# Block inverse of the delta rule: the plain inverse as DVE's 32x32 block transpose of the transposed one

## The reference, cut to what matters

```python
a_strict = jnp.where(strict, jnp.einsum("bhncd,bhnmd->bhncm", kb, k) * decay, 0.0)
lower = jnp.eye(c, dtype=f32) + a_strict
rhs = jnp.concatenate([vb, kb * jnp.exp(g)[..., None]], axis=-1)
sol = lax.linalg.triangular_solve(lower, rhs, left_side=True, lower=True, unit_diagonal=True)
```

## Time and profile before

| | |
|---|---|
| profiled execution | 1562.33 us, span 1560.4 us |
| median of three runs | 1563.34 us |
| TensorE busy | 1401.4 us (90%) |
| DVE busy | 588.0 us (38%) |
| ScalarE busy | 301.3 us (19%) |
| GpSimd busy | 361.2 us (23%) |
| mean HBM traffic | 293 GB/s |
| mean granted TensorE clock | 0.955 of full |

### The profile page before, as it was taken

One profiled execution on the slowest core, in us unless ns is written; L12 is line 12 of the kernel. 1 busy time (PEld: TensorE's weight loads), 2 busy tenths in 40 slices (PEclk: granted clock), 3 DMA queues, 4 the chain that ended last, 5 costly groups with the idle time before them and its releaser, 6 DMA issues.

```text
span 1560.4 us, 33996 instructions
## 1 busy us (share of the span) xinstructions
PE 1401.4 (90%) x13302; PEld 661.4 (42%) x13303; DVE 588.0 (38%) x1331; ACT 301.3 (19%) x563; POOL 361.2 (23%) x421
## 2 busy tenths in 40 slices
PE   6998898979938999999999999989899988889982
PEld 3445555555413444444344443434333343334441
DVE  2688877753253222223222232222222223222231
ACT  3113232031211111112112121121111211111122
POOL 5001000010012123333223232222232223222332
PEclk9999999978958999999999999999999999999996
DMA  9212000040168799999999999999999999999995
GB/s 307 70 55 78 3 28 1 1 164 1 49 238 290 285 370 372 392 410 408 403 396 405 407 405 405 395 405 408 410 401 398 410 408 405 401 408 404 409 385 145
DMA packets 110262, 457.76 MB, mean 293 GB/s; under 512 B 15140, under 2 KB 36132, under 8 KB 77430
## 3 DMA queue, kind: packets, MB, share of 16 engines
q1 hardware_dynamic: 86566, 427.88, 68.6%
q0 software_dynamic: 20592, 27.68, 7.5%
q10 hardware_dynamic: 3072, 1.76, 0.4%
HBM read 439.05 MB, written 18.22 MB: 293 GB/s over the span
## 4 chain that ended last, share of the span: by engine, by line
PE 67%; DMA 12%; DVE 10%; SPq 6%; issue 2%; ACT 2%; POOL 0%; ACTq 0%; DVEq 0%; POOLq 0%
PE bank L1840 29%; PE bank L1882 15%; DMA ring<-in_w_gate_up_dram 11%; PE bank L1528 5%; PE bank L1702 4%; PE bank L1908 3%; SPq L369 3%; SPq L374 3%; PE bank L1812 2%; DVE dslots L973 2%; PE bank L1593 1%; DVE qkbuf L997 1%; PE bank L1523 1%; PE bank L1801 1%; PE bank L1601 1%
## 5 line engine op out<-in xcount | busy, mean ns | idle before, releaser
L1840 PE MATMUL bank<-ring,wq 128*32 128x512 f32 x5184 | 588.2, 607 | 38.3 <-DMA ring<-in_w_gate_up_dram 35.8
L1840 PEld LDWEIGHTS bank<-ring,wq 128*32 128x32 f32 x5184 | 163.7, 112 | 412.6 <-issue 411.8
L1882 PE MATMUL bank<-dslots,intra 128*32 128x256 f32 x5056 | 301.6, 381 | 4.4 <-issue 1.9
L1882 PEld LDWEIGHTS bank<-dslots,intra 128*32 128x32 f32 x5056 | 169.1, 110 | 117.3 <-issue 30.2
L856 ACT ACTIVATE wq<-bank 128x512 f32<-128x512 f32 x128 | 66.1, 602 | 626.5 <-PE bank L1840 626.5
L540 POOL DMA_INDIRECT acc_rows<-rows,idx_out x83 | 153.8, 1854 | 45.8 <-POOL idx_out L530 25.6
L1411 DVE TENSOR_TENSOR intra<-bank,small 128x256 f32<-128x256 f32 x128 | 45.3, 416 | 291.8 <-PE bank L1908 259.7
L1528 PE MATMUL bank<-hbuf,ring 128*128 128x512 f32 x320 | 147.2, 600 | 0.0
L1336 DVE TENSOR_TENSOR small<-consts,bank 128x4 f32<-128x4 f32 x34 | 5.4, 159 | 327.0 <-PE bank L1801 327.0
L530 POOL COPY idx_in<-idx 128x4 int32 (+1 forms) x34 | 6.3, 186 | 448.8 <-PE bank L1812 386.1
L535 POOL DMA_INDIRECT wq<-xn_rows,idx_in x88 | 88.1, 1001 | 45.4 <-POOL idx_in L530 27.5
(11 more groups left out here) (279 smaller groups left out, 1105.7 us busy)
## 6 DMA issues: line engine op xcount, KB each, us to landing
ring<-in_w_gate_up_dram SPq DMA_DIRECT2D x256, 1024.0 KB
dslots<-in_w_down_dram SPq DMA_DIRECT2D x124, 1024.0 KB
ring<-in_w_in_dram SPq DMA_DIRECT2D x12, 1024.0 KB
ring<-in_w_out_dram SPq DMA_DIRECT2D x4, 1024.0 KB
ring<-in_w_down_dram SPq DMA_DIRECT2D x4, 1024.0 KB
rows<-in_x_dram SPq DMA_DIRECT2D x4, 512.0 KB, 7.5
hbuf<-in_x_dram SPq DMA_DIRECT2D x4, 512.0 KB, 4.9
xn_rows<-convbuf POOLq DMA_DIRECT2D x4, 512.0 KB, 4.4
```

The source lines that it names most:

```text
L1840: ins = M(bank[g][GROUP * j:GROUP * (j + 1), :], xT[:, g, c % 2, (c // 2) * GROUP:(c // 2 + 1) * GROUP], w[:, :, j * QD:(j + 1) * QD], sta ...
L1882: ins = M(b[GROUP * j:GROUP * (j + 1), col:col + QD], actT[:, g, c % 2, (c // 2) * GROUP:(c // 2 + 1) * GROUP], w[:, cc, j * QD:(j + 1) * QD],
```

## The change

After the change one of the two forms of the inverse is always the DVE block transpose of the other: one instruction over the 128x512 buffer, which transposes each 32x32 block where it stands. XT at the start is the transpose of X (so step 4, TensorE's transpose of Am and the two DVE instructions at L1031 and L1033 are gone); at levels 2 to 16 X is the transpose of the new XT (so the product at L1599 and the subtraction at L1044 are gone). The wait of TensorE for X moves from the Am' XT product to the update product. Without step 4, the SiLU job of a head's first slot stands behind step 3 in DVE's queue instead of before it.

```diff
--- before.py
+++ after.py
@@ -309,6 +309,7 @@
             LAST_TILE[u] = max(LAST_TILE.get(u, 0), i)
         LAST_TILE[NU - 2] = LAST_TILE[NU - 1] = NT - 1
         GDN_STEPS = 16
+        XX_STEPS = 2 * len(LEVELS) - 1
         PER_SLOT = [5, 5, 6]
 
         def gdn_of(s):
@@ -1025,15 +1026,7 @@
                                        in1=sq[b], op0=ALU.mult, op1=ALU.mult).then_inc(norm_ready, 1)
 
             def level(h, s):
-                if s == 1:
-
-                    dve.wait_ge(p_done, 6 * h + 1)
-                    own.mark(V.tensor_tensor(Pm, view(bank[5], 0, T, P), bcm(lmask[1]), ALU.mult))
-                    own.settle()
-                    V.scalar_tensor_tensor(out=XT, in0=Pm, scalar=-1.0, in1=bcm(ident), op0=ALU.mult,
-                                           op1=ALU.add).then_inc(xx_ready, 1)
-                    return
-                dve.wait_ge(p_done, 6 * h + LEVELS.index(s) + 1)
+                dve.wait_ge(p_done, 5 * h + LEVELS.index(s))
                 V.tensor_tensor(Pm, view(bank[5], 0, T, P), bcm(lmask[s]), ALU.mult).then_inc(p_ready, 1)
 
             def level_x(h, s):
@@ -1041,7 +1034,9 @@
                 dve.wait_ge(xx_done, 5 * h + k)
                 V.tensor_tensor(XT, XT, view(bank[7], 0, T, P), ALU.subtract).then_inc(xx_ready, 1)
                 if s < LEVELS[-1]:
-                    V.tensor_tensor(X, X, view(bank[6], 0, T, P), ALU.subtract).then_inc(xx_ready, 1)
+
+                    dve.wait_ge(xx_ready, XX_STEPS * h + 2 * k + 1)
+                    V.transpose(X[:, :, :], XT[:, :, :]).then_inc(xx_ready, 1)
 
             def gdn(h, k):
                 if k == 0:
@@ -1085,6 +1080,8 @@
                     own.settle()
                     V.scalar_tensor_tensor(out=X, in0=X, scalar=-1.0, in1=bcm(ident), op0=ALU.mult,
                                            op1=ALU.add).then_inc(xx_ready, 1)
+                    dve.wait_ge(xx_ready, XX_STEPS * h + 1)
+                    V.transpose(XT[:, :, :], X[:, :, :]).then_inc(xx_ready, 1)
                 if k == 3:
                     dve.wait_ge(kv_turned, h + 1)
                     bct = lambda v: v[:, :, h:h + 1].to_broadcast([P, T, P])
@@ -1093,8 +1090,6 @@
                     own.mark(V.tensor_tensor(uval[:, h, :, :], view(bank[4], 0, T, P), bct(betah), ALU.mult))
                     own.settle()
                     dve.sem_inc(kv_ready, 1)
-                if k == 4:
-                    level(h, 1)
                 if 5 <= k < 15:
                     s = LEVELS[1 + (k - 5) // 2]
                     if k % 2 == 1:
@@ -1117,7 +1112,7 @@
                 if s >= 2:
                     if 0 in steps:
 
-                        steps = [0, 1, 2, 4, 3]
+                        steps = [0, 1, 2, 3]
                         jobs = [jobs[0], lambda: None, lambda: None, jobs[2], lambda: norm(s - 2), tap(1)]
                     elif steps:
                         jobs[1] = tap(1)
@@ -1550,7 +1545,7 @@
                     pe.wait_ge(bias_ready, 1)
                 if k == 0:
                     if h >= 1:
-                        pe.wait_ge(xx_ready, 11 * h)
+                        pe.wait_ge(xx_ready, XX_STEPS * h)
                     for t in range(T):
                         ins = M(bank[7][:, t * P:(t + 1) * P], gg[:, t, h:h + 1].to_broadcast([P, P]), triu,
                                 start=True, stop=True)
@@ -1576,33 +1571,26 @@
                     for t in range(T):
                         ins = TR(bank[4][:, t * P:(t + 1) * P], vT[:, t * P:(t + 1) * P], ident)
                     ins.then_inc(kv_turned, 1)
-                if k == 4:
+                if k == 5:
                     pe.wait_ge(a_ready, h + 1)
-                    for t in range(T):
-                        ins = TR(bank[5][:, t * P:(t + 1) * P], Am[:, t, :], ident)
-                    ins.then_inc(p_done, 1)
-                if k == 5:
                     pe.wait_ge(in_ready, h + 1)
                     pe.wait_ge(egb_ready, h + 1)
                 if 5 <= k < 15:
                     lv = 1 + (k - 5) // 2
-                    s = LEVELS[lv]
                     if k % 2 == 1:
-                        pe.wait_ge(xx_ready, 11 * h + 2 * lv)
+                        pe.wait_ge(xx_ready, XX_STEPS * h + (2 if lv == 1 else 2 * lv - 1))
                         for t in range(T):
                             ins = M(bank[5][:, t * P:(t + 1) * P], Am[:, t, :], XT[:, t, :], start=True, stop=True)
                         ins.then_inc(p_done, 1)
                     else:
+                        pe.wait_ge(xx_ready, XX_STEPS * h + 2 * lv)
                         pe.wait_ge(p_ready, 5 * h + lv)
-                        if s < LEVELS[-1]:
-                            for t in range(T):
-                                M(bank[6][:, t * P:(t + 1) * P], Pm[:, t, :], X[:, t, :], start=True, stop=True)
                         for t in range(T):
                             ins = M(bank[7][:, t * P:(t + 1) * P], X[:, t, :], Pm[:, t, :], start=True,
                                     stop=True)
                         ins.then_inc(xx_done, 1)
                 if k == 15:
-                    pe.wait_ge(xx_ready, 11 * h + 11)
+                    pe.wait_ge(xx_ready, XX_STEPS * h + XX_STEPS)
                     pe.wait_ge(kv_ready, h + 1)
                     pe.wait_ge(rs_ready, min(2 * (h + 1) + 2, 2 * H))
                     for t in range(T):
```

## The result

The changed kernel took 1545.98 us (median of four runs, 1543.04 to 1547.54) against 1563.62 for the kernel before beside it: ratio 0.9891, interval 0.9879 to 0.9904. The forecast was 1546.5; its distance of 0.5 us is smaller than the spread of the four runs. Its profiled execution took 1547.54 us with a span of 1545.4.

A forecast was written before the change was run, and what follows sets the result against it. Bound: a ping-pong over the TensorE and DVE queues, neither full, memory no limit. Three heads at 11.3 us and head 3 at 5.6 give 16.9 us off 1562.33, so 1545.4; forecast for the median 1546.5, range 1542 to 1556.

The forecast's parts named there:

- What bounds the stage: TensorE and DVE queues wait for each other; an edit is worth only what it takes from the leg ending last.
- Price of a transpose: Each DVE transpose was taken at 0.69 us, from neighbouring 128x512 instructions, between bounds of 0.48 and 1.34.
- First slot and level 2: Heads 0 to 2: 1.21 us gained in all, less 0.40 for GpSimd holding up a DVE instruction.
- Level 4: Heads 0 to 2: 1.49 us gained, the X product's 0.89 and 0.60 for L1044, both on the chain.
- Level 8: Heads 0 to 2: 0.60 us gained from L1044; the removed TensorE product worth nothing, since DVE's queue is late.
- Level 16: Heads 0 to 2: 0.86 us gained, 0.26 left of the X product's 0.89 plus 0.60 for L1044.
- Level 32: Heads 0 to 2: no gain, since there was no X product there before the change.
- Head 3: 5.6 us gained: 1.49 each at levels 2, 4 and 16, 0.60 at level 8, 0.5 in the first slot.
- Sum: 3.76 us a head, 11.3 us for heads 0 to 2, and 5.6 in head 3: total 16.9 us.
- Behind the stage: Everything behind shifts by the same amount; the rival, gain given back in the expert loop, 1563 us, had chance 0.05.
- the dearer transpose: Rival: transposes at 1.34 us lose 7.8 us, at three places a head where DVE ends last; 1554.3 us, chance 0.14.
- The clock: Rival: TensorE's clock falls once a head, some 3 us each, so 12 us go back; 1558 us, chance 0.09.

The follow-up runs named there:

- e_product: Changed kernel with the X product put back on TensorE ahead of the update product at levels 2 to 16, read by nothing; 1553.49 us, ratio 0.9968.
- e_wait: Kernel before, with only TensorE's wait for X moved from the Am' XT product to the update step, no transpose; 1552.78 us, ratio 0.995.
- e_silu: Changed kernel with the first slot's SiLU job back ahead of step 3; 1546.61 us, ratio 0.9899 against the kernel before.
- e_again: The changed kernel timed once more, nothing altered; 1544.60 us, ratio 0.9905 against the kernel before.
- e_double: Changed kernel with each of the twenty transposes done twice, the second waiting for the first; 1552.33 us, ratio 0.9954 against the kernel before.
- e_taps_silu: Changed kernel with the second slot's three taps moved to other places and SiLU back ahead of step 3; 1536.10 us, ratio 0.984.
- e_conv: Changed kernel with conv4 of a head's first slot moved behind step 2, the start of X; 1549.92 us, ratio 0.9927.
- e_start: Kernel before with only the start changed: XT by transpose of X, step 4 gone, SiLU behind step 3, levels as before; 1560.17 us, ratio 1.0009.
- e_taps: Changed kernel with the three taps ahead of level 8's subtraction moved to other places, none removed; 1539.78 us, ratio 0.9849.
- e_conv_silu: Changed kernel with taps moved and, in the first slot, conv4, one tap and SiLU in that order ahead of step 3; 1534.45 us, ratio 0.9847.
- e_both: Changed kernel with the first slot's conv4 behind step 2 and the three taps moved as well; 1542.79 us, ratio 0.987.

## Why the prediction was right

- **What bounds the stage**: right. Removing TensorE work paid only in legs that end on it: the product is worth 0.89 at levels 4 and 16 and nothing at level 8 (e_product), where DVE's queue ended the leg. Of the stage's 17.2 us the moved wait alone gives 7.7 (e_wait); the rest needed the transposes.
- **Price of a transpose**: 0.69 taken, 0.711 measured. The estimate from the Trainium skill (VectorE: DVE Perf Modes, "The three transpose paths"), 0.71, was the closer one: the trace agrees with it, float32 and all.
- **First slot and level 2**: 1.21 less 0.40 forecast, 1.02 measured (0.58 and 0.44). The late squares and the new wait came as described, 1.23 us instead of 1.5, and the hold-up of conv4's first instruction was 0.18 and not 0.40 (e_silu takes it back). The 0.43 for L1582 stands in no row shown: its row has 0.66, and the next instruction starts 0.50 behind it; nothing but the work taken away and head 3's 0.5 (0.48 measured) hangs on it.
- **Level 4**: 1.49 forecast, 1.49 measured.
- **Level 8**: 0.60 forecast, 0.56 measured, all of it L1044 (e_wait 0.60, e_product nothing).
- **Level 16**: 0.86 forecast, 0.82 measured, and the working does not carry the number. The starts that it compares, 4.09 and 3.74, leave 0.54 of the 0.89, not 0.26, and 3.74 is a start on the chain, later than the instruction's own. Before, by TensorE's timeline:

```profile
207.44 1.16 PE L1593 MATMUL bank<-dslots 128*128 128x128 f32 x8 [1.78 <-DVE dslots L1044]
...
211.01 1.05 PE L1599 MATMUL bank<-dslots 128*128 128x128 f32 x8
211.90 1.06 PE L1601 MATMUL bank<-dslots 128*128 128x128 f32 x8
```

So XT's product started 4.46 us behind L1593, and after the change 4.17 (201.89 to 206.06): 0.29 are left, of which 0.07 goes because the group takes 1.13 us instead of 1.06 with a wait in front of it. With L1044's 0.60 that makes the 0.82; that the forecast came so near was luck. Taken one by one the parts differ, since the mask behind conv4 is the late event: L1044 off the path is worth 0.05 (e_wait), the product behind the mask its full 0.89 (e_product), and DVE's longer queue with the transpose costs 0.12 (6.97 against 6.85).

- **Level 32**: nothing forecast, 4.55 before and after.
- **Head 3**: 5.6 forecast, 5.55 measured. **Sum**: 16.9 forecast, 17.2 in the stage.
- **Behind the stage**: shifted as a whole (1245.4 before, 1246.2 after), so nothing was given back there beyond the spread between executions. That the medians differ by 17.6 us here and by 15.5 in e_again, around a forecast of 16.9, says how near a hit can be taken: the terms were right to some tenths, the last half microsecond of the total was luck.
- **Rivals**: the dearer transpose fell with the 0.711, though its places and size were near (e_double: 10.4 us for twice the price). The clock did not cost in the profiled execution of the changed kernel, but the rival was not empty, and the prediction's sign against itself, a clock below 1 inside of heads, did show in head 0 (0.94). A fall cost 1 us twice in e_again, and some 1.2 us in head 0 of e_taps_silu. I had argued against it from the longest wait of head 1's walk, 2.3 us, against 2.0 in the kernel before. The row says 1.8 there; after the change it is 2.02, and head 0, which I had taken to be like head 1, has a wait of 3.42 before its first product (2.20 in e_again). The runs show that the length does not decide alone. The 3 us for a fall had no row behind it; the runs show 0 to 1.6, which is why the forecast stands even with it.

## What to carry to other kernels

Where two engines hand work to each other, an operation that one of them does beside the path is cheap there even if it is no faster: here 0.71 us of DVE took the place of 0.89 us of TensorE and 0.60 of DVE. Find the late event of each leg before pricing an edit: at level 16 what stands behind it counted in full (0.89 us), and what stands ahead of it next to nothing (0.05). Look at the waits by themselves too: a wait that named more than its reader needs held 7.7 of the 17.2 us. After the change read the waits again: moving three taps of filler a head gave another 7.4 us of stage, 0.4 of what the change gave, and no new instruction.

## What was not expected of the hardware

One single wait of TensorE, and how long the instructions behind it took. Eight matmuls of L1583 take 1.05 to 1.16 us at full clock, the two sums of squares 1.02 to 1.13:

| wait, us | clock fell right behind it or one group later | it did not |
|---|---|---|
| 2.01 or 2.02, x8 | 1.87 (e_again, head 1), 1.91 (e_conv, head 0); one group later in head 0 of e_again and of e_double | 1.16 (after and e_silu, three heads each; e_again, head 2; e_double and e_conv, heads 1 and 2) |
| 2.20 to 2.36, x8 | 2.02 and 1.20 (e_double, heads 1 and 2) | 1.13 (e_again, e_start and e_taps, head 0) |
| 2.22, x2 | 1.31 (e_conv_silu, head 2) | 1.10 (e_conv_silu, head 1) |
| 3.42 to 4.15, x8 | 1.93 to 2.05 (after, e_silu, e_product, e_taps_silu and e_double, head 0) | none seen |
| 2.97 to 3.64, x2 | 2.07 (e_conv, head 1), 1.85 (e_both, head 1), 1.86 (e_conv_silu, head 0); one group later in head 0 of e_conv and head 2 of e_both | 1.12 (e_conv, head 2; e_both, head 0) |

The falls that came one group later are seen only in the group behind, as in e_both, head 2:

```profile
228.23 1.12 PE L1545 MATMUL bank<-sqbuf,consts 128*128 128x512 f32 x2 [3.14 <-POOL sqbuf L491]
229.19 1.69 PE L1594 MATMUL bank<-dslots 128*128 128x128 f32 x8
```

So the same wait, within one kernel and at one place, sometimes lowered the clock and sometimes not. The Trainium skill (TensorE: Matmul & The Clock Gate, "HAM oscillation - how this bites in real kernels") warns that waits between bursts of matmuls can do this. The trace agrees in part: some of the waits in the table lowered the clock, others of the same length did not. Where DVE did not cover it a fall cost 1.0 to 1.6 us; it cost 0.2 to 0.3 in head 2 of e_conv_silu and head 0 of e_double, and nothing in heads 1 and 2 of e_double and in head 0 of the profiled execution of after (44.35 us against 44.38 for head 1). What decides between the two outcomes stays open: no run varied the work around a wait of fixed length.

The other one is the meeting of DVE and GpSimd: conv4's first instruction took 0.66 or 0.67 us beside GpSimd's square in heads 0 and 1 of the kernel after, and 1.35 in the first slot beside a GpSimd mask, as in the earlier trace rows. In e_conv L1060 took 1.48 us there instead of 0.42. The price of such a meeting is not one number; I had charged 0.40, and it was 0.18.
